# Attention with stacked value halves, and its diagonals and bias tables made by GpSimd

## The reference, cut to what matters

```python
s = jnp.einsum('bnqgrd,bnkgd->bngrqk', qb, kw) * ATTN_SCALE
bias = -slopes[...] * distance                 # first mixer; the second reads rel_bias
p = jax.nn.softmax(jnp.where(mask, s + bias, NEG_INF), axis=-1)
o = jnp.einsum('bngrqk,bnkgd->bnqgrd', p, vw)
```

## Time and profile before

| what | value |
|---|---|
| median of 3 runs | 2441.55 us (2435.31 to 2442.39) |
| the profiled execution | 2440.35 us, of which 2438.6 us are its span |
| granted TensorE clock, mean | 0.985 |
| attention of the first mixer | 501 to 665 us of the span |
| attention of the second mixer | 1118 to 1146 us and 1182 to 1210 us |

### The profile page before, as it was taken

How to read it: one execution, slowest core, us unless ns; L and a number is a source line. 1 busy time by engine, 2 the same in 40 slices (tenths; PEclk the granted TensorE clock), 3 DMA queues, 4 the chain that set the end, 5 groups by cost and what they waited for, 6 DMA issues and landing times.

```text
span 2438.6 us, 36915 instructions
## 1 busy us (share of the span) xinstructions
PE 2367.6 (97%) x13960; PEld 1944.9 (80%) x13960; DVE 1196.3 (49%) x1967; ACT 910.0 (37%) x1442; POOL 1070.0 (44%) x551
## 2 busy tenths in 40 slices
PE   8999999999899999998999989999999999999998
PEld 7888888878888888876777777888888887888887
DVE  5441246278844331375544554731733995741732
ACT  5331234456653321245554323322223435321222
POOL 5444445530044444432264443444444993444442
PEclk9999999999999999999999999999999998999999
DMA  4332233400023322222110002332222232322321
GB/s 160 102 95 95 95 95 106 136 18 1 1 87 104 94 103 92 97 95 69 61 53 28 28 29 63 102 95 95 95 95 88 87 113 69 101 98 93 96 88 59
DMA packets 56124, 200.08 MB, mean 82 GB/s; under 512 B 6224, under 2 KB 6480, under 8 KB 56016
## 3 DMA queue, kind: packets, MB, share of 16 engines
q1 hardware_dynamic: 54432, 195.82, 24.8%
q10 hardware_dynamic: 1584, 2.75, 0.4%
HBM read 196.45 MB, written 2.10 MB: 81 GB/s over the span
## 4 chain that ended last, share of the span: by engine, by line
PE 63%; issue 21%; POOL 11%; DVE 3%; ACT 2%; DMA 0%; POOLq 0%; ACTq 0%; DVEq 0%
PE ps L129 19%; PE ps L131 19%; PE ps L130 18%; POOL sb_w_lo L110 8%; POOL sb_caway L2411 1%; PE ps L1632 1%; PE ps L1629 1%; PE ps L1618 1%; POOL sb_level L2098 1%; PE ps L628 0%; PE ps L1592 0%; DVE ps L2462 0%; PE ps L613 0%; DVE sb_t_p L705 0%; POOL sb_cu_lo L2423 0%
## 5 line engine op out<-in xcount | busy, mean ns | idle before, releaser
L110 POOL TENSOR_TENSOR sb_w_lo<-sb_w_raw,sb_w_hi 128x1024 fp32r<-128x1024 f32 x362 | 891.9, 2467 | 1191.8 <-ACT sb_w_hi L97 1191.0
L129 PE MATMUL ps<-sb_xn_hi,sb_w_hi 128*128 128x512 f32 (+1 forms) x1688 | 666.4, 395 | 5.2 <-POOL sb_w_lo L110 3.1
L130 PE MATMUL ps<-sb_xn_lo,sb_w_hi 128*128 128x512 f32 (+1 forms) x1688 | 658.9, 390 | 0.0
L131 PE MATMUL ps<-sb_xn_hi,sb_w_lo 128*128 128x512 f32 (+1 forms) x1688 | 658.5, 390 | 0.0
L97 ACT ACTIVATE sb_w_hi<-sb_w_raw 128x1024 fp32r<-128x1024 f32 x362 | 379.7, 1055 | 487.4 <-PE ps L131 460.3
L129 PEld LDWEIGHTS ps<-sb_xn_hi,sb_w_hi 128*128 128x128 f32 (+1 forms) x1688 | 316.8, 188 | 77.8 <-issue 5.6
L131 PEld LDWEIGHTS ps<-sb_xn_hi,sb_w_lo 128*128 128x128 f32 (+1 forms) x1688 | 317.2, 188 | 68.0
L130 PEld LDWEIGHTS ps<-sb_xn_lo,sb_w_hi 128*128 128x128 f32 (+1 forms) x1688 | 317.2, 188 | 67.0 <-issue 1.7
L131 PE MATMUL ps<-sb_hid_hi,sb_w_lo 128*128 128x512 f32 x864 | 344.2, 398 | 0.0
L129 PE MATMUL ps<-sb_hid_hi,sb_w_hi 128*128 128x512 f32 x864 | 339.6, 393 | 1.8 <-DVE sb_hid_lo L397 1.8
L130 PE MATMUL ps<-sb_hid_lo,sb_w_hi 128*128 128x512 f32 x864 | 340.3, 394 | 0.0
(11 more groups left out here) (435 smaller groups left out, 3046.4 us busy)
## 6 DMA issues: line engine op xcount, KB each, us to landing
sb_w_raw<-weights SPq DMA_DIRECT2D x365, 512.0 KB, 3.5
sb_stage<-x SPq DMA_DIRECT2D x4, 512.0 KB, 5.2
sb_abias<-table ACTq DMA_DIRECT2D x8, 256.0 KB, 2.7
out<-sb_out_stage SPq DMA_DIRECT2D x8, 256.0 KB, 2.8
sb_lora_w<-lora ACTq DMA_DIRECT2D x2, 256.0 KB, 2.7
sb_par<-params SPq DMA_DIRECT2D x1, 231.0 KB, 6.5
sb_ctaps<-dw ACTq DMA_DIRECT2D x1, 124.0 KB, 3.7
```

The source lines that it names most:

```text
L110: pool.tensor_tensor(c.w_lo[:, slot, 0:width], c.w_raw[:, slot, 0:width], c.w_hi[:, slot, 0:width].bitcast(F32), ALU.subtract).then_inc(c. ...
L129: pe.matmul(out, hi, rhs_hi(k0 + k), start=first, stop=False)
L130: pe.matmul(out, hi, rhs_lo(k0 + k), start=False, stop=False)
L131: mm = pe.matmul(out, lo, rhs_hi(k0 + k), start=False, stop=last)
```

## The change

**Values.** The value tile of one head is 64 columns wide. Before, the stationary tile of a product was 128 columns of two heads, high or low, and the half that belongs to the other head was computed and not used. Now a stationary tile holds for one head the high part in one half of its columns and the low part in the other. Two products (with the high and with the low part of the probabilities) replace three, and the output bank has the high half and the low half of the sum on different rows. ACT copies the low half to the other rows (`moved`), DVE adds it to the high half (`whole`), and for the first mixer POOL makes the high and low part of the output.

**Diagonals and bias tables.** A new program `attention_pool` makes the diagonals and the bias tables on POOL, and the parts of `rwkv_constants` are dealt out between its steps, one in every second step. **Order on DVE.** A step is now scale(n+1), maxima(n+2), low(n), outputs(n-1).

The core of the diff (left out: the same edits for the other tables, semaphore names, and the value tiles of the second mixer):

```diff
         if p.opens and p.o_before > 0:
-            pe.wait_ge(a.s_olow, p.o_before)
+            pe.wait_ge(a.s_osum, p.o_before)
...
-            for v, w_part in ((p.v_hi, a.pt_hi), (p.v_hi, a.pt_lo), (p.v_lo, a.pt_hi)):
-                mm = pe.matmul(out[:, q0 * P:q1 * P], v(key), w_part[rows, n % 2, w], start=first,
-                               stop=p.closes and x == len(p.kind.turned) - 1 and v is p.v_lo, skip_group_check=True)
+            for w_part in (a.pt_hi, a.pt_lo):
+                mm = pe.matmul(out[:, q0 * P:q1 * P], p.v(key), w_part[rows, n % 2, w], start=first,
+                               stop=p.closes and x == len(p.kind.turned) - 1 and w_part is a.pt_lo, skip_group_check=True)
...
         for side in range(2):
-            rows = slice(side * HD, side * HD + HD)
-            if a.o32 is not None:
-                act.activation(a.o32[rows, p.tile], c.ps[rows, O_BANK + side], ACT.Copy).then_inc(a.s_olow, 1)
-                continue
-            act.activation(a.o_hi[rows, p.tile], c.ps[rows, O_BANK + side], ACT.Copy).then_inc(a.s_ohigh, 1)
+            act.activation(a.moved[half_rows(side)], c.ps[half_rows(1 - side), O_BANK + side], ACT.Copy).then_inc(a.s_moved, 1)
...
-            p.prepare_dve(dve)
+        dve.wait_ge(*p.biased)
...
     def scale(n):
-        nonlocal sinks
-        p = passes[n]
+        p, step = passes[n], steps[n]
         dve.wait_ge(a.s_exp, TT * n + TT)
...
+        if n >= 2:
+            dve.wait_ge(a.s_scaled, TT * (n - 1))
+        dve.reciprocal(a.scale[:, n % 2], a.sums[:, n % 2]).then_inc(a.s_scale, 1)
+        step += 1
...
-
-        for i in range(TT):
-            dve.tensor_scalar(a.diagonal[:, n % 2, i], c.ident[:], a.scale[:, n % 2, i:i + 1], None,
-                              ALU.mult).then_inc(a.s_scaled, 1)
...
+        pairs = pairs_before(passes, n)
+            rows = half_rows(side)
+            dve.wait_ge(a.s_moved, 2 * pairs + side + 1)
+            dve.tensor_tensor(whole[rows], c.ps[rows, O_BANK + side], a.moved[rows], ALU.add).then_inc(a.s_osum, 1)
+
     maxima(0)
     for n in range(-1, len(passes)):
+        if n + 1 < len(passes):
+            scale(n + 1)
         if n + 2 < len(passes):
             maxima(n + 2)
         if n >= 0:
             low(n)
-        if n + 1 < len(passes):
-            scale(n + 1)
         if n >= 1:
             outputs(n - 1)
+    outputs(len(passes) - 1)
...
+def attention_pool(pool, c, a, passes, between=None):
+    n_banks = passes_before(passes)
+    def diagonal(n):
+        pool.wait_ge(a.s_scale, steps[n + 1])
+        if n >= 2:
+            pool.wait_ge(a.s_turned, n_banks[n - 1])
+        for i in range(TT):
+            pool.tensor_scalar(a.diagonal[:, n % 2, i], c.ident[:], a.scale[:, n % 2, i:i + 1], None,
+                               ALU.mult).then_inc(a.s_scaled, 1)
+
+    def outputs(n):
+        p = passes[n]
+        if not p.pair_done or a.o32 is not None:
+            return
+        pairs = pairs_before(passes, n)
+        pool.wait_ge(a.s_osum, 2 * pairs + 2)
+        pool.tensor_copy(a.o_hi[:, p.tile], a.whole).then_inc(a.s_ohigh, 1)
+        pool.wait_ge(a.s_ohigh, pairs + 1)
+        pool.tensor_tensor(a.o_lo[:, p.tile], a.whole, a.o_hi[:, p.tile].bitcast(F32), ALU.subtract).then_inc(a.s_olow, 1)
+
+    prepare(0)
+    prepare(1)
+    for n in range(-1, len(passes)):
+        if n + 1 < len(passes):
+            diagonal(n + 1)
+        prepare(n + 3)
+        if n >= 1:
+            outputs(n - 1)
+        if between is not None:
+            between(n)
     outputs(len(passes) - 1)
...
+
+    return ap.rearrange("p (t s n) -> p t s n", s=2, n=HD)
+
+
+def high_part(v):
+
+    return v.rearrange("p t s (h n) -> p t (s h) n", n=HD)[:, :, 0:4:3]
+
+
+def low_part(v):
+
+    return v.rearrange("p t s (h n) -> p t (s h) n", n=HD)[:, :, 1:3]
+
+
...
+        def prepare(pool, h=h, slot=slot, x=x):
+            if x >= 2:
+                pool.wait_ge(a.s_max, TT * (3 * x - 3))
+            else:
+                pool.wait_ge(*((m.s_unit, 1) if x == 0 else (m.s_gates, 1)))
+            pool.tensor_scalar(m.bias_cmp[:, slot], c.dist_cmp[:], -SLOPES[h] / SCALE, None, ALU.mult).then_inc(a.s_bias, 1)
+            pool.tensor_scalar(m.bias[slot][:], c.dist[:], -SLOPES[h] / SCALE, None, ALU.mult).then_inc(a.s_bias, 1)
...
-            for part in range(CONSTANT_PARTS):
-                rwkv_constants(pool, c, part)
+
+            def constants(n):
+                if n >= 2 and n % 2 == 0 and n // 2 <= CONSTANT_PARTS:
+                    rwkv_constants(pool, c, n // 2 - 1)
+
+            attention_pool(pool, c, a, passes, constants)
             conv, own = B["pw1"], B["rwkv_in"] + 12
-            stream_low(pool, c, split, own + 5)
+            stream_low(pool, c, split, own + RING - 7)
+            attention_pool(pool, c, ta, att_passes(c, ta, t, 0))
+            stream_low(pool, c, own + RING - 7, own + RING - 1)
+            attention_pool(pool, c, tb, att_passes(c, tb, t, 1))
+            stream_low(pool, c, own + RING - 1, own + 5)
             rwkv_pool(pool, c, w, own)
```

More of the change, by code:

```diff
@@ L580, in passes_before, with scale_steps, pairs_before, half_rows @@
     return out
+def scale_steps(passes):
+    out = [0]
+    for p in passes:
+        out.append(out[-1] + 1 + (p.sink is not None) + (p.gate is not None) + (p.row_mask is not None))
+    return out
+def pairs_before(passes, n):
+    return sum(p.pair_done for p in passes[:n])
+def half_rows(side):
+    return slice(side * HD, side * HD + HD)
 def attention_pe(pe, c, a, passes):
@@ L692, in attention_dve @@
     n_banks = passes_before(passes)
-    pairs = 0
-    sinks = 0
+    steps = scale_steps(passes)
     def maxima(n):
         p = passes[n]
-        if p.prepare_dve is not None:
-            p.prepare_dve(dve)
+        dve.wait_ge(*p.biased)
         if n >= 3:
@@ L743, in outputs @@
     def outputs(n):
-        nonlocal pairs
         p = passes[n]
-        if not p.pair_done or a.o32 is not None:
+        if not p.pair_done:
             return
+        pairs = pairs_before(passes, n)
+        whole = a.whole if a.o32 is None else a.o32[:, p.tile]
+        if a.o32 is None and pairs:
+            dve.wait_ge(a.s_olow, pairs)
         for side in range(2):
-            rows = slice(side * HD, side * HD + HD)
-            dve.wait_ge(a.s_ohigh, 2 * pairs + side + 1)
-            dve.tensor_tensor(a.o_lo[rows, p.tile], c.ps[rows, O_BANK + side], a.o_hi[rows, p.tile].bitcast(F32),
-                              ALU.subtract).then_inc(a.s_olow, 1)
-        pairs += 1
-    passes_gated = [sum(q.gate is not None for q in passes[:n + 1]) for n in range(len(passes))]
-    passes_masked = [sum(q.row_mask is not None for q in passes[:n + 1]) for n in range(len(passes))]
+            rows = half_rows(side)
+            dve.wait_ge(a.s_moved, 2 * pairs + side + 1)
+            dve.tensor_tensor(whole[rows], c.ps[rows, O_BANK + side], a.moved[rows], ALU.add).then_inc(a.s_osum, 1)
     maxima(0)
     for n in range(-1, len(passes)):
+        if n + 1 < len(passes):
+            scale(n + 1)
         if n + 2 < len(passes):
@@ L762, in attention_dve, with prepare @@
             low(n)
-        if n + 1 < len(passes):
-            scale(n + 1)
         if n >= 1:
             outputs(n - 1)
+    outputs(len(passes) - 1)
+def attention_pool(pool, c, a, passes, between=None):
+    n_banks = passes_before(passes)
+    steps = scale_steps(passes)
+    def prepare(n):
+        if n < len(passes) and passes[n].prepare is not None:
+            passes[n].prepare(pool)
+    def diagonal(n):
[24 more added lines that the diff above has]
+            between(n)
     outputs(len(passes) - 1)
@@ L774, in attention_buffers @@
     a.diagonal = c.y[:, 0:2].rearrange("p a (t n) -> p a t n", n=P)
+    a.moved, a.whole = c.y[:, 2], c.ss[:]
     if pt is None:
@@ L792, in attention_view @@
     b.o_hi, b.o_lo, b.o32 = a.o_hi, a.o_lo, o32
[L793 removed]
+    b.p, b.diagonal, b.pt_hi, b.pt_lo, b.moved, b.whole = a.p, a.diagonal, a.pt_hi, a.pt_lo, a.moved, a.whole
     b.maxima, b.negmax, b.sums, b.scale, b.sink_exp = a.maxima, a.negmax, a.sums, a.scale, a.sink_exp
```

111 lines of the change are left out of this document (53 added, 58 removed).

## The result

The changed kernel takes 2447.11 us in the median of ten runs (2443.91 to 2452.41), the kernel before 2441.32 us in ten (2435.28 to 2442.39). The ratio is 1.0032, with a 95% interval of 1.0021 to 1.0043: slower by 0.3%, a little under the 7.3 us that the prediction took for the least change that can be told, clear of noise all the same, and inside its range. (The ratio compares all runs of both kernels and isn't the quotient of the two medians, which is 1.0024.) The profiled execution is the slowest of the ten, 2452.41 us. Of its distance to the profile before, 12.1 us, the first mixer holds most.

What follows compares the result with a forecast made beforehand. TensorE was taken to set the beat in most steps, VectorE behind output pairs and in LOCAL passes. Terms -6.9+0.8-1.4+5.7+1.0+2.2+0 made +1.4 us, forecast 2442 us, range 2431 to 2454.

Steps and rivals of the forecast that it cites:

- the likeliest case: Whole kernel: no change that can be told, 2434 to 2449 us; chance 0.46.
- Two heads, rings alone: First mixer: two heads take 27.2 us for 29.1, four times, -7.6 us, taken as -6.9.
- GpSimd's lateness with the slow clock: Diagonals late behind output parts and selects at steps 6, 12, 18: +5.7 us; slow transposes after idling: +1.0.
- VectorE held beside GpSimd: First mixer: negation, 32 times in the ring, slower while GpSimd works: +2.2 us (0 to 10).
- third rival: VectorE held by GpSimd once a pass in the first mixer: 9.9 us instead of 2.2, 2450 us; chance 0.27, clock included.
- LOCAL passes: First mixer's LOCAL passes: a pair takes 10.7 us for 10.5, four pairs, +0.8 us.
- Tail: End of the pass list: no maxima follow, diagonals off VectorE, values of two passes shorter: -1.4 us.
- Second mixer: Both halves of four passes: 0 in all (-1.5 to +1.5 us).
- first rival: The work that goes is what counts: about 2421 us, or 2432 for a half of it; chance of either 0.27.

Runs made afterwards that it cites:

- e2: The changed kernel with GpSimd's two output parts made one step later, behind the diagonals: 2441.3 us, ratio 1.0006 to the kernel before.
- e8: The changed kernel with one edit, ScalarE's copies of the output halves ahead of the exponentials: 2434.4 us, ratio 0.9982 to the kernel before.
- e5: As e2, with the eleven parts of the constants moved out of attention into the later projections: 2435.8 us, ratio 0.9987 to the kernel before.
- e7: As e5, with the four diagonals of a pass made by one GpSimd multiplication: 2438.4 us, ratio 0.9992 to the kernel before.
- e6: As e5, with ScalarE's copies of the output halves ahead of the exponentials: 2426.4 us, ratio 0.9943 to the kernel before.
- e10: As e6, with the diagonals back on VectorE in the order of before: 2425.8 us, ratio 0.9942 to the kernel before.
- e3: The changed kernel with the edits of e1 and e2 together: 2449.0 us, ratio 1.0038 to the kernel before.
- e1: The changed kernel with the parts of the constants moved to steps not behind an output pair: 2445.4 us, ratio 1.0024 to the kernel before.

## Why the prediction came out as it did

The time lies in the range, and the likeliest case was no change: 2442 against 2447.1, at 0.3% the edge to slower. The mechanisms named were there. Of the sum, most terms came out on the slow side (first mixer +1.4 forecast, +9.6 in the two traces), and what kept the time inside was the width of the range more than the sum. Term by term:

- **Two heads, rings alone.** Right in the number: 27.2 forecast, 27.1 measured once GpSimd was in time (e2). The period of 27 us never shows in the changed kernel, since each pair of heads has a late diagonal in it. The wait for the exponentials is there: VectorE's scale waits for ScalarE in 20 of 32 passes. Two parts of the working were off. A head without outputs takes 12.54 us with TensorE never idle, and half of TensorE's 24.7 is 12.35: the 1.16 us that the sum takes off is idle time of the weight loads, and the products behind them waited 0.75 us only, which gives 25.1, twice 12.54:

```profile
605.28 2.47 PE L613 MATMUL ps<-sb_y,sb_a_p 128*128 128x128 f32 x20 [0.75 <-DVE sb_y L732]
```

  And behind a pair TensorE stands 1.30 us at a value product, for the bank that the adds free; the sum had the adds only in the way of the scale. That 27.2 and 27.1 agree so well is in part luck.
- **GpSimd's lateness with the slow clock**, 5.7 + 1.0 us: the mechanism, the chain and the three places were right; the size was not. Two heads of 33.0, 29.4 and 31.3 us are 12.3 us over three times 27.1, with VectorE's hold, the next term, in part inside. Three sizes were off: the diagonal (0.59 for 0.40 us; the row chosen was a quarter of a 128x512 multiplication, and the price of a small one isn't a quarter), the slow transposes behind each stall (2.1, 1.0 and 2.4 us over 2.5, against 1.0 in all), and pass 6, which waited 1.18 us for diagonals behind part 1 (0.84 and twice 0.17), at a place where the prediction let GpSimd release nothing. The prediction had GpSimd release every step from 0.6 us a diagonal on; at 0.59 it doesn't, and that was close.
- **VectorE held beside GpSimd**, 2.2 us: negations (308 - 183) x 32 = 4.0 us and gates (254 - 169) x 24 = 2.0 us, so operations longer by 6.0 us in sum, of which no run isolates what they cost. The third rival's mechanism is real, at some 60% of its 9.9. It depends on what stands beside what: with GpSimd's output parts a step later (e2) the negation takes 228 ns but the gate 295, with GpSimd's program as it was and ScalarE's copies moved (e8) 216 and 280, and with the selects gone too (e5) 198 and 222. At 545.85 us a negation of 0.77 us ends at 546.62, as the subtraction of L803 (545.32 and 1.28 us) ends at 546.60. The Trainium skill states such a hold in "SBUF — State Buffer", section "Who interferes with whom", for instructions of VectorE with two SBUF inputs or in a two-port mode, and excludes others; the trace agrees for the gate, with two inputs, and for the maxima, with one input from PSUM, which took 686 ns for 685 before in their widest form. Whether the negation, with one input, runs in a two-port mode no run here shows. In e7 a negation beside a table of 1.49 us was held 0.36 us and not to its end, so not every pair of operations goes by it.
- **LOCAL passes**, +0.8 us: +1.8 from pass 21 to 31. The forecast of 10.7 us a pair was 11.3 in the pair shown. Here, and behind the FULL pairs, was the larger chance that the prediction passed by: it priced the copies and adds between exponentials and scale, 2.71 + 1.41 us, and took their order as given.
- **Tail**, -1.4: from the last transposes to the next projection 4.3 us for 4.9, so -0.6. **Second mixer**, 0: -0.5.
- **The first rival** (the work that goes is what counts) is what e6 and e10 come near, at 2426 for its 2421: with output parts, constants and copies in other places the change is worth 14 us. The row that decided against it was the order of ScalarE's program and not a limit of an engine.

What stays open: why e3's median lies 3.6 us over e1's, though in its trace passes 3 to 21 take 88.6 us and in e1's 91.7; and how much of the spread of 8 us over one kernel's runs is the clock at the entry. Three traces with the same instructions up to pass 5 took 18.4 (changed kernel), 13.2 (e2) and 14.8 us (e8) from pass 0 to pass 3; that speaks for the clock, and no run isolates it.

## What to carry to other kernels

When work moves to another engine, write out its queue between the last thing that it waits for and the first thing that is waited for: side work costs most there and here cost nothing in the projections, and moving it by a step can move the stall with it. Before pricing such a chain, ask which links could stand in another order: one swap on ScalarE, with no work removed, was worth 12.7 us, where the diagonals' move was worth nothing that can be told once the swap was made. The same swap was worth nothing in the kernel before, so such a price holds for one order only. A gain in the bounding engine's work, like the stacked values, was worth more when no other queue was late (12.3 us against 7.4), so measure it by putting the work back.
